# A hybrid decoder layer: the weight splits moved ahead of the steps of their slot

## The reference

```python
h = rms_norm(x, norm_g)
proj = jnp.einsum('bsd,de->bse', h, w_in)
# A: 12 heads, softmax attention over three dilated windows, mixed by their denominators
out_a = dilated_mixture(qa, ka, heads_a(av))
# B: 8 heads, causal softmax attention with a decaying bias c[t] - c[s]
out_b = forgetting_attention(qb, kb, heads_b(bv), log_f)
# C: 4 heads, gated linear attention: S_t = diag(alpha_t) S_{t-1} + k_t^T v_t, o_t = q_t S_t
out_c = rms_norm(gla_chunked(qc, kc, vc, log_a), gla_out_gain)
mixed = concatenate([out_a * silu(az), out_b * silu(bz), out_c * silu(cz)])
return x + jnp.einsum('bse,ed->bsd', mixed, w_out)
```

## Time and profile before

| | |
|---|---|
| median of 3 runs | 2222.88 us (2222.19 to 2222.98) |
| profiled execution, its own time | 2222.88 us |
| its span, first to last instruction | 2221.2 us |
| TensorE busy | 2145.2 us, 97% |
| VectorE busy | 998.9 us, 45% |
| ScalarE busy | 862.3 us, 39% |
| GpSimd busy | 247.8 us, 11% |
| granted TensorE clock, mean | 0.987 of full speed |
| splits in the groups, VectorE L1172 | 224, 191.3 us |
| splits in the groups, ScalarE L779 | 224, 138.9 us |

### The profile page before, as it was taken

One profiled execution on the slowest core, in us unless ns is written; L12 is line 12 of the kernel. 1 busy time (PEld: TensorE's weight loads), 2 busy tenths in 40 slices (PEclk: granted clock), 3 DMA queues, 4 the chain that ended last, 5 costly groups with the idle time before them and its releaser, 6 DMA issues.

```text
span 2221.2 us, 30415 instructions
## 1 busy us (share of the span) xinstructions
PE 2145.2 (97%) x11016; PEld 1817.6 (82%) x11016; DVE 998.9 (45%) x1639; ACT 862.3 (39%) x1466; POOL 247.8 (11%) x141
## 2 busy tenths in 40 slices
PE   6999999999989999999999999999999968899999
PEld 5788888888878888888888888888888857778887
DVE  6611356363634544445454545445454555522122
ACT  7311234434344544444444445444444444311110
POOL 0000143241411000101000000001010000000000
PEclk9999999999999999999999999999999979999999
DMA  6322324233322222222222222222232154333234
GB/s 216 79 70 77 91 76 106 59 99 101 80 74 83 72 85 72 74 62 82 66 71 74 62 86 81 91 62 90 74 97 72 59 180 151 119 124 100 71 126 144
DMA packets 190459, 203.23 MB, mean 91 GB/s; under 512 B 16169, under 2 KB 139097, under 8 KB 189233
## 3 DMA queue, kind: packets, MB, share of 16 engines
q1 hardware_dynamic: 173664, 171.80, 26.3%
q10 hardware_dynamic: 16720, 30.45, 3.7%
HBM read 152.38 MB, written 49.83 MB: 91 GB/s over the span
## 4 chain that ended last, share of the span: by engine, by line
PE 85%; DVE 4%; ACT 4%; DMA 4%; issue 2%; SPq 0%; ACTq 0%; DVEq 0%
PE acc L1619 18%; PE acc L1621 17%; PE acc L1620 17%; PE turned L1813 3%; PE pv L1826 3%; PE pv L1825 3%; PE scores L1802 2%; PE scores L1799 2%; DMA w_raw<-in_w_out_dram 1%; PE pv L1707 1%; DMA w_raw<-in_w_in_dram 1%; PE acc L1905 1%; PE acc L1907 1%; PE acc L1906 1%; PE side L1707 1%
## 5 line engine op out<-in xcount | busy, mean ns | idle before, releaser
L1619 PE MATMUL acc<-act_hi,w_hi 128*128 128x512 f32 x1856 | 739.8, 399 | 14.5 <-DVE w_lo L1172 9.8
L1621 PE MATMUL acc<-act_hi,w_lo 128*128 128x512 f32 x1856 | 726.7, 392 | 0.0
L1620 PE MATMUL acc<-act_lo,w_hi 128*128 128x512 f32 x1856 | 725.2, 391 | 0.0
L1619 PEld LDWEIGHTS acc<-act_hi,w_hi 128*128 128x128 f32 x1856 | 350.2, 189 | 86.4 <-DVE w_lo L1172 13.3
L1621 PEld LDWEIGHTS acc<-act_hi,w_lo 128*128 128x128 f32 x1856 | 349.6, 188 | 76.7
L1620 PEld LDWEIGHTS acc<-act_lo,w_hi 128*128 128x128 f32 x1856 | 350.3, 189 | 67.2
L1172 DVE TENSOR_TENSOR w_lo<-w_raw,w_hi 128x512 fp32r<-128x512 f32 x224 | 191.3, 854 | 345.3 <-ACT w_hi L779 345.3
L1056 ACT ACTIVATE prob<-prob,neg_max 128x128 f32<-128x128 f32 (+7 forms) x160 | 124.4, 778 | 278.0 <-DVE neg_max L1445 278.0
L1461 DVE TENSOR_TENSOR pt_lo<-turned,pt_hi 128x128 fp32r<-128x128 f32 (+7 forms) x160 | 121.2, 757 | 243.5 <-ACT pt_hi L1064 241.9
L779 ACT ACTIVATE w_hi<-w_raw 128x512 fp32r<-128x512 f32 x224 | 138.9, 622 | 125.9 <-PE acc L1621 102.4
L1064 ACT ACTIVATE pt_hi<-turned 128x128 fp32r<-128x128 f32 (+7 forms) x160 | 104.3, 652 | 191.7 <-PE turned L1813 191.1
(11 more groups left out here) (266 smaller groups left out, 2812.5 us busy)
## 6 DMA issues: line engine op xcount, KB each, us to landing
w_raw<-in_w_in_dram SPq DMA_DIRECT2D x240, 256.0 KB, 2.9
proj_scratch<-stage ACTq DMA_DIRECT2D x116, 256.0 KB, 2.1
w_raw<-in_w_out_dram SPq DMA_DIRECT2D x94, 256.0 KB, 3.1
raw<-proj_scratch SPq DMA_DIRECT2D x20, 512.0 KB, 3.2
raw<-mixed_scratch SPq DMA_DIRECT2D x16, 512.0 KB, 4.4
res<-in_x_dram SPq DMA_DIRECT2D x24, 256.0 KB, 5.6
out_dram<-res SPq DMA_DIRECT2D x24, 256.0 KB, 3.0
sq<-proj_scratch SPq DMA_DIRECT2D x10, 512.0 KB, 4.3
```

What stands on the lines that cost most here:

```text
L1619: pe.matmul(acc, hi, xh, start=first, stop=False)
L1620: pe.matmul(acc, hi, xl, start=False, stop=False)
L1621: mm = pe.matmul(acc, lo, xh, start=False, stop=end)
```

## The change

In `group` on both engines the two splits of an even slot now stand ahead of that slot's steps, and on ScalarE also ahead of the copy at slot 7 (which is an odd slot, so nothing changes there). No instruction is added or removed, TensorE's, GpSimd's and SyncE's lists stay as they are, and so do all waits.

```diff
--- before.py
+++ after.py
@@ -828,11 +828,11 @@
 
             def group(s, row, steps):
                 for slot in range(8):
+                    if slot % 2 == 0:
+                        split_hi(s, slot // 2 + 1)
                     if slot == 7:
                         evac(s, 0)
                     steps(slot)
-                    if slot % 2 == 0:
-                        split_hi(s, slot // 2 + 1)
                 evac(s, 1)
                 save(s, row)
 
@@ -1174,9 +1174,9 @@
 
             def group(s, steps):
                 for slot in range(8):
-                    steps(slot)
                     if slot % 2 == 0:
                         split_lo(s, slot // 2 + 1)
+                    steps(slot)
 
 
             def split_lo_half(n, kq):
```

## The result

| | before | after |
|---|---|---|
| median | 2222.53 us (6 runs, 2221.08 to 2222.98) | 2240.27 us (6 runs, 2237.53 to 2242.48) |
| ratio | | 1.0079, 95% interval 1.0067 to 1.009 |
| profiled execution, own time | 2222.88 us | 2238.91 us |
| its span | 2221.2 us | 2237.2 us |
| mean granted clock | 0.987 | 0.984 |

The changed kernel is 0.8% slower: 17.7 us by the medians, 16.0 by the two spans. It was forecast at 2233 with 2223 to 2246 around it. From here on "+" is time by which TensorE does the same instruction later than in the trace of before, read from the starts of its matmuls.

A forecast was written before the change was run, and what follows sets the result against it. TensorE was taken as the bound, busy without a gap in the pairs. From 2222.9 us, -11.8 + 10.6 + 1.7 + 4.4 + 5.6 = +10.5 gave 2233 us, range 2223 to 2246, the likeliest case 2228 to 2241.

The forecast's parts named there:

- gain at slots 20 to 23: End of each GLA head: earlier w_lo removes TensorE's wait at slot 22; -11.8 us over four heads.
- wait before level 0: Each GLA head: differences behind slot 6's split, TensorE waits 1.6 to 2.1 us, 1.65 taken; +6.6 in all.
- waits at later levels: Later even levels of each head hang on their slot's split; 1.0 us a head taken, bounds 0 and 2.
- lower clock behind these waits: Heads: one of four waits followed by the lower clock, +1.7 us, bounds 0 and 6.8.
- slots 0 and 1 of the pairs: Pairs 1 to 8: v_st behind w_lo without margin, a wait of 0.55 us each; +4.4 us.
- slots 16 and 17: All nine pairs: mask, neg_max and sq_lo behind split and w_lo, TensorE waits 0.5 to 0.7 us; +5.6 us.
- slot 28: Pairs: neg_max for slot 28 still 0.2 to 0.35 us ahead of TensorE; no loss.
- seam before the pairs, tail: First group of the pairs hangs on transfers, last pair with output projection does not change; 0 us.
- Port: Rival: pairs' k_hi copy, held by GpSimd, delays slots 3 and 27, 0.9 us each; +16, 2249; chance 0.12.
- Faster alone: Rival: level chain keeps its lead, gain at slot 22 stands alone; 2211, or 2216 with half pair losses; chance 0.07.
- even: Rival: gain and level losses cancel, pairs cost 7 to 10 us; +2 to +5, 2225 to 2228; chance 0.15.
- slot 22 stays: Rival: wait at slot 22 of the heads stays, the split waiting for something else; sum +22, 2245; chance 0.02.

The follow-up runs named there:

- number 4: Only the splits of slot 20 of each GLA head ahead of their steps, both engines, against the kernel before: 2212.73 us, ratio 0.9952.
- number 10: Only the two splits of slot 6 of the GLA heads ahead of their steps, against the kernel before: 2232.62 us, ratio 1.0036.
- number 9: The whole change except slot 6 of the GLA heads, whose splits stay behind the steps, against the kernel before: 2236.85 us, ratio 1.0057.
- number 2: The change in the groups of the GLA heads alone, on both engines, against the kernel before: ratio 1.0002.
- number 5: Only the two splits of slot 0 of the pairs ahead of their steps, against the kernel before: ratio 1.0029, 6.4 us.
- number 6: Only the two splits of slot 16 of the pairs ahead of their steps, against the kernel before: ratio 1.0027, 6.0 us.
- number 7: Only the two splits of slot 26 of the pairs ahead of their steps, against the kernel before: ratio 1.0001.
- number 8: Slot 26's two splits in the pairs moved ahead, and GpSimd's product q_st also waits for VectorE's copy of k_hi, against the kernel before: ratio 0.9999.

## Why the prediction was right, point by point

The direction, the mechanism and the range were right. The sizes, in us of the profiled executions:

| step | forecast | measured | shown by |
|---|---|---|---|
| gain at slots 20 to 23 | -11.8 | -11.4 | trace after; alone -9.8, number 4 |
| wait before level 0 | +6.6 | +6.2 | trace after, number 10 |
| waits at later levels | +4.0 | 0 | trace after; number 9 |
| lower clock behind these waits | +1.7 | +6.7 | trace after, numbers 2 and 10 |
| slots 0 and 1 of the pairs | +4.4 | +6.35 | number 5 |
| slots 16 and 17 | +5.6 | +6.1 | number 6 |
| slot 28 | 0 | +1.5 | rest of the pairs' 13.9; in part the port, 7 and 8 |
| seam before the pairs, tail | 0 | -0.7, +1.2 | trace after, not tested |
| sum | +10.5 | +16.0 | |

The two rows of the clock and of the wait before level 0 are 12.9 together; by the starts of the matmuls they divide into 6.8 and 6.1, with the 0.16 of each wait counted to the wait.

- **Gain.** Right in size. One step of it was wrong: w_lo was to be there "before 430", 3.5 ahead of its use, and came at the last moment (0.4 too late in number 4), held for 4 us. The same holding that was weighed for the copy of k_hi applied here, and I did not look at what GpSimd does at slot 20 (in the trace of before its product runs from 428.61 for 4.60). It cost next to nothing here by luck of the length: with the product 0.4 later, as in number 4, it costs 0.4 a head.
- **Level 0.** A wait of 1.6 to 2.1 was forecast, 1.55 measured. The chain of durations from the earlier trace rows held.
- **Later levels.** The step that failed: I took 1.0 for each head as if it came on top. The wait itself is real (1.56 at level 2 when level 0 does not wait, number 9), but level 2's chain starts as TensorE's stop before level 0 does (in the changed kernel ScalarE's copy at 375.00, two stores, the split at 376.33), so that stop gives the chain as much time as it takes. The chain's own sum was off too: the split comes 2.5 and not 0.28 behind TensorE at slot 8 (375.05 against 372.54 in number 9), since level 1's exponential and the copy and stores of the finished group stand ahead of it on ScalarE.
- **Clock.** The largest miss. I expected one fall in four waits, there were four. The upper bound of 6.8 is just above the 6.7.
- **Slots 0 and 1.** 0.55 was forecast for each pair, 0.7 came: the idle time is 0.49, and TensorE's matmul starts 0.65 later than without it. And there are nine, not eight: pair 0 waits 0.53 as well.
- **Slots 16 and 17.** A pair loses 0.55 to 0.75, against 0.5 to 0.7 in the forecast. The waits themselves are 0.38 to 0.49, less than the 0.5 to 0.7 that were to show it.
- **Port.** A rival with 2249 on it. The Trainium skill's page SBUF — State Buffer, section "Who interferes with whom", says of VectorE and GpSimd instructions that contend for their shared ports that whichever issues first keeps them to its end and the other blocks. Three places agree: the copy with 2.76 behind the product and 0.69 ahead of it, and w_lo with 4.69 behind L741. Not all of it can be seen here: the product that issued first took 2.67 in number 7 and 2.39 in number 8, where no copy waited for it. The rival's price was ten times too high or more (16 against at most 1.5 in all of the pairs' rest), since the held time fell into idle time, as the argument against it had said.
- **Faster alone, even, slot 22 stays.** All three are out: level 0 waits, the pairs lose 13.9 and not 0 to 10, and the wait at slot 22 is gone.

That the sum came out within 5.5 of the two traces (7.3 by the medians) is partly luck: the later levels, 4.0 too high, cover most of the clock's 5.0.

## What to carry to other kernels

Moving work that one engine owes to the bottleneck ahead of its other steps is only worth it at the slots where that work is late today; here slot 20, one of the 24 of a head, carried nearly all of the gain (10 us of 11.4), slots 6 and 8 of the heads and 0, 16 and 26 of the pairs made the steps behind the split late, and slot 22 of the heads and thirteen slots of the pairs changed nothing. Price each slot by what stands behind the moved instruction on each engine, and by what GpSimd has running when it starts. Two delays that hit the bottleneck one after the other need not add: where the steps of the second one's chain run on during the first stop, that stop gives them time.

## What the runs showed of the hardware

- A stop of TensorE of 1.55 us was followed by a stretch at the lower level of the clock in 4 of 4 heads of the changed kernel, in 2 of 4 of number 2, whose lists in the heads are the same, and in 3 of 4 of number 10, and it cost about 1.7 or 3.4 us each time; stops of 0.5 us in the pairs had none (granted clock 1.00 from 1000 to 1300 us in the changed kernel). The length of the stop alone doesn't decide it: one of 1.60 at slot 22 of head 0 was not followed by such a stretch in any of the eight traces that have it. The other three heads stop there for 1.96 to 1.98, and the lower level followed two of these three stops in seven of the traces and one in the eighth (number 10).
- A VectorE split of 128x512 took 4.69 us instead of 0.69 beside a GpSimd product of 96x2048 that had started 0.47 earlier. I had reckoned with 1.9; in the heads of the trace of before the longest is 2.46.
